# One-core transformer kernel on Trainium2: the first five projection blocks on the unnormed input, scaled in PSUM, and another order of the first transfers

## The reference, cut to what matters

```python
def rms_norm(x, w):
    xf = x.astype(jnp.float32)
    y = xf * lax.rsqrt(jnp.mean(xf * xf, axis=-1, keepdims=True) + EPS)
    return (y * w.astype(jnp.float32)).astype(x.dtype)

def mamba2_mixer(h, norm_w, in_w, conv_w, conv_b, dt_bias, a_log, d_skip, gnorm_w, out_w):
    b, s, _ = h.shape
    u = rms_norm(h, norm_w)
    zxbcdt = u @ in_w
    z, xbc, dt = jnp.split(zxbcdt, [D_INNER, D_INNER + CONV_CH], axis=-1)
    xbc = lax.conv_general_dilated(xbc, conv_w[:, None, :], window_strides=(1,),
    ...
    xbc = jax.nn.silu(xbc)
    ...
    dt = jax.nn.softplus(dt.astype(jnp.float32) + dt_bias.astype(jnp.float32))
    a = -jnp.exp(a_log.astype(jnp.float32))
    y = ssd_chunked(xs, dt, a, bm, cm)
```

## Time and profile before

| | |
|---|---|
| median of three runs | 1540.54 us (1541.24, 1516.41, 1540.54) |
| the profiled execution | 1513.08 us |
| its span | 1511.2 us |
| mean granted TensorE clock | 0.971 |
| PE busy | 1413.0 us |
| DVE, ACT, POOL busy | 817.0, 649.1, 659.5 us |

### The profile page before, as it was taken

How to read it: one execution, slowest core, us unless ns; L and a number is a source line. 1 busy time by engine, 2 the same in 40 slices (tenths; PEclk the granted TensorE clock), 3 DMA queues, 4 the chain that set the end, 5 groups by cost and what they waited for, 6 DMA issues and landing times.

```text
span 1511.2 us, 18102 instructions
## 1 busy us (share of the span) xinstructions
PE 1413.0 (94%) x6802; PEld 1114.1 (74%) x6802; DVE 817.0 (54%) x1358; ACT 649.1 (43%) x1090; POOL 659.5 (44%) x319
## 2 busy tenths in 40 slices
PE   5989999999999999789999999988989999999996
PEld 4877878777678788556887888664558788888775
DVE  4535564757566734664675311356646554455656
ACT  4634524535444534584554311444544332332452
POOL 3443453535334544355544334323244455555441
PEclk9999999999999999999999999988999999999998
DMA  4221222222223233110323343120003233333331
GB/s 160 86 70 56 84 71 77 77 70 69 72 70 97 71 98 92 35 56 29 92 90 114 96 137 128 56 71 1 1 1 98 84 98 98 98 98 98 98 94 60
DMA packets 33366, 118.92 MB, mean 79 GB/s; under 512 B 3964, under 2 KB 4348, under 8 KB 33024
## 3 DMA queue, kind: packets, MB, share of 16 engines
q1 hardware_dynamic: 31680, 113.26, 24.2%
q10 hardware_dynamic: 1600, 4.50, 0.9%
HBM read 115.65 MB, written 2.10 MB: 78 GB/s over the span
## 4 chain that ended last, share of the span: by engine, by line
PE 76%; DVE 10%; ACT 8%; issue 4%; POOL 2%; ACTq 0%; DMA 0%; DVEq 0%
PE bank L1153 73%; DVE arena L1817 2%; PE bank L1535 1%; ACT wsh L786 1%; ACT arena L1087 1%; ACT sq L749 1%; POOL wsl L641 1%; DVE h L1818 1%; ACT arena L917 1%; POOL arena L720 1%; PE bank L1389 1%; DVE arena L1813 1%; DVE arena L1656 1%; DVE arena L1637 1%; DVE arena L2125 0%
## 5 line engine op out<-in xcount | busy, mean ns | idle before, releaser
L641 POOL TENSOR_TENSOR wsl<-ring,wsh 128x1024 fp32r<-128x1024 f32 x199 | 482.8, 2427 | 670.9 <-ACT wsh L786 670.9
L786 ACT ACTIVATE wsh<-ring 128x1024 fp32r<-128x1024 f32 x199 | 210.3, 1057 | 557.7 <-PE bank L1153 513.6
L1153 PE MATMUL bank<-parts0h,wsh 128*128 128x512 f32 x744 | 301.4, 405 | 15.2 <-DVE small L1920 4.4
L1153 PE MATMUL bank<-parts0h,wsl 128*128 128x512 f32 x744 | 292.9, 394 | 0.0
L1153 PE MATMUL bank<-parts0l,wsh 128*128 128x512 f32 x744 | 292.9, 394 | 0.0
L1153 PE MATMUL bank<-parts1h,wsh 128*128 128x512 f32 x688 | 275.0, 400 | 6.7 <-POOL parts1l L641 3.1
L1153 PE MATMUL bank<-parts1l,wsh 128*128 128x512 f32 x688 | 269.5, 392 | 0.0
L1153 PE MATMUL bank<-parts1h,wsl 128*128 128x512 f32 x688 | 269.4, 392 | 0.0
L1153 PE MATMUL bank<-arena 128*64 128x128 f32 (+10 forms) x1008 | 168.2, 398 | 28.8 <-DVE arena L2165 7.9
L1153 PEld LDWEIGHTS bank<-parts0h,wsh 128*128 128x128 f32 x744 | 141.7, 190 | 55.2 <-issue 10.2
L1153 PEld LDWEIGHTS bank<-parts0l,wsh 128*128 128x128 f32 x744 | 141.9, 191 | 31.0 <-issue 2.6
(11 more groups left out here) (279 smaller groups left out, 1870.8 us busy)
## 6 DMA issues: line engine op xcount, KB each, us to landing
ring<-in_wstream SPq DMA_DIRECT2D x210, 512.0 KB, 3.6
arena<-in_alibi ACTq DMA_DIRECT2D x2, 1024.0 KB, 5.1
outT<-arena SPq DMA_DIRECT2D x8, 256.0 KB, 2.1
h<-in_xT SPq DMA_DIRECT2D x2, 512.0 KB, 6.1
h<-in_xT ACTq DMA_DIRECT2D x2, 512.0 KB, 6.3
arena<-in_cmpb ACTq DMA_DIRECT2D x1, 496.0 KB
con<-in_con ACTq DMA_DIRECT2D x1, 390.5 KB
rowb<-in_rowb ACTq DMA_DIRECT2D x1, 184.0 KB
```

Source lines behind the costliest of these rows:

```text
L641: return nc.gpsimd.tensor_tensor(dst, src, hi.bitcast(F32), ALU.subtract)
L786: nc.scalar.activation(wsh[n % NSET][:, :], src, ACT.Copy).then_inc(*done("high", ("high", L)))
L1153: return nc.tensor.matmul(*args, **kw)
```

## The change

Blocks p00, p01, dt, p02 and p03 no longer use the normed input. ACT and DVE split `h * norm weight` straight into pair 1 (step `raw`), PE multiplies these, and the factor is put on the product: DVE multiplies the PSUM bank in place by `rtb0`, a copy of the spread factor in SBUF, before the convolution or the copy to `dtf` reads it. The matmuls of the five blocks stand at new steps `("L", ...)` ahead of the old ones; what ACT and DVE do with the products stays at the old steps. The squares, the column sums and the spread of the factor follow behind or between these blocks, and the normed input is made in two halves (`("hn", "ssm", 0)` and `1`), first used by p04. The first two weight blocks get their low part from DVE, not POOL. The first transfers are reordered: on ACT's queue `vec` goes first, then two quarters of the input; on SP's queue weight block 0, then the other two quarters, then the stream. The copies `identr` and `laterr` move to the step `cum`, behind p03, since they lie in pair 1.

```diff
--- before.py
+++ after.py
@@ -91,6 +91,10 @@
 VERSION_OF = {"ssm": 0, "ple0": 1, "kv": 2, "attn": 2, "ple1": 3, "ln1": 4, "ln2": 5, "ple2": 6, "final": 7}
+RAW = [("proj", 0, 0), ("proj", 0, 1), ("dtl",), ("proj", 0, 2), ("proj", 0, 3)]
+LATER = RAW + [("upg", 0), ("upv", 0)]
 def pipeline(x, units, closing):
...
@@ -116,7 +120,8 @@
 def steps():
-    out = [("load",), ("norm", 0), ("first_weights",), ("nb", 0), ("hn", "ssm")]
+    out = [("first_weights", 0), ("raw",), ("first_weights", 1), ("load",)] + [("L", *x) for x in RAW[:2]]
+    out += [("norm", 0), ("nb", 0), ("hn", "ssm", 0), ("L", *RAW[2]), ("hn", "ssm", 1)] + [("L", *x) for x in RAW[3:]]
     proj = {g: [("proj", g, i) for i in range(10)] for g in range(GROUPS)}
     sout = {g: [("sout", g, m) for m in range(KD)] for g in range(GROUPS)}
     out += proj[0][:2] + [("dtl",), proj[0][2], ("dt",), proj[0][3], proj[0][4], ("cum",)] + proj[0][5:7] + [("angles",)] + proj[0][7:]
...
@@ -392,7 +397,7 @@
 def splits_at(step):
     if step[0] == "first_weights":
-        return [(b, SPLITNO[b]) for b in SPLIT[:NSET]]
+        return [(SPLIT[step[1]], step[1])]
...
@@ -615,12 +624,11 @@
         @block.sync
         def _(sp):
-            for m in range(0, KD, 4):
-                sp.dma_start(h[:, m:m + 2, :], ins["xT"][:, m:m + 2, :])\
-                    .then_inc(*done(f"xin{m}", ("h", 0, m), ("h", 0, m + 1), inc=16))
-            sp.wait_ge(*at("h", 0, 4))
             for L, b in enumerate(BLOCKS):
+                if L == 1:
+                    for m in range(2, KD, 4):
+                        sp.dma_start(h[:, m:m + 2, :], ins["xT"][:, m:m + 2, :])\
+                            .then_inc(*done(f"xin{m}", ("h", 0, m), ("h", 0, m + 1), inc=16))
...
@@ -722,19 +730,21 @@
         @block.scalar
         def _(act):
-            for m in range(2, KD, 4):
+            act.dma_start(vec[:, :], ins["vec"]).then_inc(*done("vec_in", ("vec",), inc=16))
+            for m in range(0, KD, 4):
                 act.dma_start(h[:, m:m + 2, :], ins["xT"][:, m:m + 2, :])\
                     .then_inc(*done(f"xin{m}", ("h", 0, m), ("h", 0, m + 1), inc=16))
-            for i, (dst, name) in enumerate([(con[:, :], "con"), (vec[:, :], "vec"), (rowb[:, :], "rowb"),
-                                             (w2c[:, :, :], "w2c"),
+            for i, (dst, name) in enumerate([(con[:, :], "con"), (rowb[:, :], "rowb"), (w2c[:, :, :], "w2c"),
                                              (peT[:, :, :], "peT"), (mbias[:, :], "mbias"), (pos[:, :], "pos")]):
-                act.dma_start(dst, ins[name]).then_inc(*done("consts", *([("consts",)] if i == 6 else []), inc=16))
+                act.dma_start(dst, ins[name]).then_inc(*done("consts", *([("consts",)] if i == 5 else []), inc=16))
...
-                    nc.scalar.activation(identr, ident, ACT.Copy)
-                    nc.scalar.activation(laterr, later, ACT.Copy).then_inc(*done("mask_parts", ("mask_parts",)))
+                if k == "raw":
+                    for m in range(KD):
+                        act.wait_ge(*at("h", 0, m))
+                        nc.scalar.activation(xgh[:, m, :], h[:, m, :], ACT.Identity,
+                                             scale=vec[:, V_NORM["ssm"] + m:V_NORM["ssm"] + m + 1])\
+                            .then_inc(*done("rawhi", ("rawhi", m)))
...
                     b = ps(step)
-                    act.wait_ge(*at("mm", *step))
+                    act.wait_ge(*at("raw_scaled" if step in RAW else "mm", *step))
...
                 if k == "cum":
+                    act.wait_ge(*at("mm", *RAW[-1]))
+                    nc.scalar.activation(identr, ident, ACT.Copy)
+                    nc.scalar.activation(laterr, later, ACT.Copy).then_inc(*done("mask_parts", ("mask_parts",)))
                     act.wait_ge(*at("mm", "lg"))
...
@@ -1166,13 +1181,17 @@
                               skip_group_check=True)
                 return last
-            def linear(job, name, src, normed=None):
+            def linear(job, name, src, normed=None, middle=None):
                 b = open_bank(job)
                 w = weights(name)
                 for kt in range(KD):
-                    if normed:
+                    if normed == "raw":
+                        pe.wait_ge(*at("raw", kt))
+                    elif normed:
                         pe.wait_ge(*at("hn", normed, kt))
+                    if middle and kt == KD // 2:
+                        middle()
                     last = mm3(b[:, :], [q[:, tok(kt)] for q in w], [q[:, kt, :] for q in src], kt == 0, kt == KD - 1)
...
                     b = open_acc(("ss", a[0]))
...
-                    b = open_acc(("rb", a[0]))
-                    pe.wait_ge(*at("ndiag", a[0]))
-                    mm(b[:, :], ones, rt[:, :], start=True, stop=True).then_inc(*done("mm", ("mm", "rb", a[0])))
-                if k == "proj":
-                    linear(step, blocks_of(step)[0], hn, "ssm" if a == (0, 0) else None)
-                if k == "dtl":
-                    linear(step, ("dt",), hn)
+                def broadcast(ver):
+                    b = open_acc(("rb", ver))
+                    pe.wait_ge(*at("ndiag", ver))
+                    mm(b[:, :], ones, rt[:, :], start=True, stop=True).then_inc(*done("mm", ("mm", "rb", ver)))
+                if k == "nb" and a[0]:
+                    broadcast(a[0])
+                if k == "proj" and step not in RAW:
+                    linear(step, blocks_of(step)[0], hn, "ssm" if a == (0, 4) else None)
...
                         linear(step, blocks_of(step)[0], hn)
-                if k == "L":
+                if k == "L" and a in RAW:
+                    linear(a, blocks_of(step)[0], xg, "raw" if a == RAW[0] else None, (lambda: broadcast(0)) if a == ("dtl",) else None)
+                if k == "L" and a not in RAW:
                     linear(a, blocks_of(step)[0], hn, "ln2" if a == ("upg", 0) else None)
...
                         .then_inc(*done("split_p", ("split", L), ("slot_free", L)))
+                if k == "first_weights":
+                    b, n = splits_at(step)[0]
+                    L = BLKNO[b]
+                    dve.wait_ge(*at("high", L))
+                    low(wsl[n % NSET][:, :], ring[:, L % NSLOT, :], wsh[n % NSET][:, :])\
+                        .then_inc(*done("split_first", ("split", L), ("slot_free", L)))
+                if k == "raw":
+                    dve.wait_ge(*at("vec"))
+                    for m in range(KD):
+                        dve.wait_ge(*at("rawhi", m))
+                        nc.vector.scalar_tensor_tensor(xgl[:, m, :], h[:, m, :], vec[:, V_NORM["ssm"] + m:V_NORM["ssm"] + m + 1],
+                                                       xgh[:, m, :].bitcast(F32), ALU.mult, ALU.subtract)\
+                            .then_inc(*done("raw", ("raw", m)))
+                if step in RAW:
+                    dve.wait_ge(*at("rtb", 0))
+                    dve.wait_ge(*at("mm", *step))
+                    nc.vector.tensor_tensor(ps(step)[:, :], ps(step)[:, :], rtb0, ALU.mult)\
+                        .then_inc(*done("raw_scaled", ("raw_scaled", *step)))
...
                             .then_inc(*done("hn_dve", ("hn", name, q)))
+                if k == "nb" and a[0] == 0:
+                    dve.wait_ge(*at("mm", "rb", 0))
+                    nc.vector.tensor_copy(rtb0, acc(("rb", 0))[:, :]).then_inc(*done("rtb", ("rtb", 0)))
...
```

More of the change, by code:

```diff
@@ L253, in jobs_of @@
         return [a]
-    if step in (("upg", 0), ("upv", 0)):
+    if step in LATER:
         return []
@@ L328, in blocks_of @@
     if k == "L":
-        return [(*a, 0)]
-    if step in (("upg", 0), ("upv", 0)):
+        k, a = a[0], a[1:]
+    elif step in LATER:
         return []
@@ L533, in build @@
         rtb = ar(38, SEQ)
+        rtb0 = ar(25, SEQ)
         rtb1 = ar(35, SEQ)
@@ L538, in build, with tiles_of @@
         hf3 = [ar(30 + b, SEQ) for b in range(4)]
+        def tiles_of(a):
+            return list(range(KD)) if len(a) == 1 else list(range(4 * a[1], 4 * a[1] + 4))
         def normed_tiles(name):
@@ L648, in _ @@
                     src = ring[:, L % NSLOT, :]
-                    if n is not None:
+                    if n is not None and k != "first_weights":
                         pool.wait_ge(*at("high", L))
@@ L653, in _ @@
                 if k == "hn" and a[0] != "final":
-                    for name in a:
+                    for name in a[:1]:
                         hi, lo = (xgh, xgl) if name == "kv" else (hnh, hnl)
                         buf = normed_tiles(name)
-                        for m in range(1, KD, 2):
+                        for m in tiles_of(a)[1::2]:
                             pool.wait_ge(*at("hnhi", name, m))
@@ L737, in link @@
                 act.wait_ge(*at("act_step", chain[0]))
+            act.wait_ge(*at("vec"))
             def square(ver, m):
@@ L804, in _ @@
                 if k == "hn" and a[0] != "final":
```

(19 more changed lines are left out.)

## The result

| | before | changed |
|---|---|---|
| first comparison, median of 4 runs each | 1528.47 us (1512.5 to 1541.24) | 1539.24 us (1537.29 to 1541.11) |
| second comparison (with r1 to e3 below) | 1517.15 us (35 runs) | 1531.39 us (12 runs) |
| fourth comparison (with r2, e8, e9) | 1523.61 us (29 runs) | 1541.33 us (12 runs) |

What follows compares the result with a forecast made beforehand. PE bounds the kernel (busy 1413.0 of 1511.2 us); an 11.0 us lead, less 9.2 us idle at the transposes and 1.8 us half pace, sums to +0.4 us: 1541 us in the upper place, range 1508 to 1546.

Steps and rivals of the forecast that it cites:

- the sum: Opening stage to p04's end: 59.4 us against 59.0 before, so +0.4 us, put on the upper place's 1540.5 us.
- the two places of the runs: Whole kernel: runs at 1516.41 or 1540.54 to 1541.24 us, by something not the change's; median forecast in the upper.
- The head: Start through p03: p00 starts at 9.9 us instead of 23.12, p03 ends at 42.6 instead of 53.6, lead 11.0 us.
- The transfers: First loads of input and weights: their new order costs nothing, since the bytes are the same.
- The transposes: After p03: PE idle for 9.2 us while ACT and DVE work one after the other towards `dtf`, leaving 1.8 us lead.
- The product in place in PSUM: DVE's products on the path to `dtf`: 0.69 us each, bounds 0.43 us and twice 0.69.
- The half pace: p04 behind the idle gap: nine matmuls at 0.43 instead of 0.227 us, 1.8 us lost, p04 ends at 59.4 us.
- the other half of the working: Behind p04: if PE kept its pace, `cum` would wait for `da` until 58.8 us, so half pace costs only 0.6 us.
- Rival A: Transposes: ACT and DVE reach `dtf` without PE's gap, the lead stays, 11 us shorter, 1529.5 us; it or half, chance 0.10.
- Rival B: Normed tiles: DVE and POOL in each other's way, POOL's block up to 3.70 us, p03 late, +2.5 us, 1543 us; chance 0.09.

Runs made afterwards that it cites:

- r1: The changed kernel rerun unaltered; 6 of 12 runs at 1540.41 to 1543.24 us, the others 1514.86 to 1522.38 us.
- e3: Changed kernel with dt's product and copy and p00's product and first tap ahead of p03; 7 of 12 runs over 1530 us, lower five median 1511.75 us.
- r2: The changed kernel rerun unaltered a third time; 8 of 12 runs over 1530 us, the four lower runs with median 1520.3 us.
- e8: Changed kernel without 24 of the 40 one-column sums of the mLSTM, denominators incomplete; median 1511.33 us, 12 runs from 1504.39 to 1512.74.
- e9: Kernel before with seven extra ACT activations ahead of the squares; 6 of 12 runs over 1530 us, the six lower with median 1520.6 us.
- e1: Changed kernel with 16 extra unread 128x512 matmuls at the start of the mLSTM product stage; median 1518.45 us, none of 12 runs over 1530.
- e2: Kernel before with 16 extra unread 128x512 matmuls at the start of the mLSTM product stage; median 1517.0 us, none of 12 runs over 1530.
- e5: Kernel before with three extra ACT activations ahead of the squares; 8 of 12 runs over 1530 us, the four lower with median 1518.6 us.
- e6: Kernel before with only the new order of the first transfers; p00 starts at 25.94 us, 2.8 later; 4 of 12 runs over 1530 us.
- e4: Changed kernel with 16 filler matmuls in the mLSTM stage and 36 more ahead of PE's wait for the transposes; median 1517.56 us, 0 of 12 over 1530.
- e7: e3's step order with 8 filler matmuls in the mLSTM stage; median 1510.93 us, ratio to the lower runs of before 0.9966.

## Why the prediction was wrong

**The step that failed** is one sentence of the sum: that the two places of the runs come "by something that the rows don't show and that isn't the change's". From it the forecast took one fixed place for both kernels, and so +0.4 us between them; the spell had no term. That it isn't the change's stands as far as the runs show; that it could be held fixed, the same on both sides, is what failed. What the runs showed in its place: the places are a spell at half pace in the mLSTM stage, 64.9 us or 3.4 us long, that each kernel falls into in some of its executions and not in others. The change's four runs all fell in the upper place, two of before's four did, and so the first comparison has the change 1.5% slower than the low runs of before, while without the spell (e1, e2) it is +1.45 us. That 1539.24 us lies only 1.8 us from the forecast is luck: four draws of four in the place that I had named.

Could the rows have shown it? In part. Before the forecast I had windows of 30 us over the whole span of before, and they read a granted clock of 0.94, 0.78, 0.78 and 0.86 between 960 and 1080 us. I used the windows of the first 100 us only, for what they meant for the change. But 90 to 120 us reads 0.89 as well, part of the low clock behind 1010 us lies beside an idle PE, and there was no trace of an upper run, so the rows gave a stage to suspect and not the cause. The two places in three runs were reason enough for a term of up to 25 us either way, with a chance.

Whether the change also makes the spell likelier is open. Over all comparisons 18 of 28 runs of the changed kernel were upper and 36 of 103 of before. Taken as independent runs that would be chance in about 1 of 100 cases; but within a comparison they share a chip, and the first four alone were what raised the question (without them 14 of 24 against 34 of 99, 1 in 27). Delays at the start (e5, e9) gave 14 of 24, the reorder e3 7 of 12, e6 with a delay of 2.8 us 4 of 12. There is no rule of the delay in these. What isn't open is that the spell needs no change to appear.

**The head** was right: 9.9 us forecast, 10.18 measured; the end of p01 23.0 (22.8), the column sums 1.7 us (1.9), p03 late by 0.5 us (0.34 us of it idle by PE's record) and its end 42.9 (42.6). In r1, r2, e1 and e8 PE stays longer at half pace at its start, and p03 ends at 43.2 to 44.4. The transfers cost nothing, as reasoned, in this kernel; e6 shows that they cost 2.8 us where the constants are wanted early.

**The transposes** were right: forecast 9.2 us of idle PE, measured 9.22. The product in place in PSUM takes 0.69 us, the row with one PSUM operand, not twice that. The same wait is 9.21 or 9.22 us in all five traces of this order. e3 shows that the queue order is the cause.

**The half pace** was mis-sized in the trace above, and the sum with it. I took nine matmuls from the start's 4.0 us. There it lasted until 58.4, thirteen matmuls at 0.43 us (not fifteen, as e4's expectation has it), and p04 took 8.3 us instead of 5.45: 2.9 us lost instead of 1.8. In r1, r2, e1 and e8 p04 took 7.0, 7.3, 8.4 and 7.1 us, so 1.8 lies inside a scatter of 1.5 to 3.0. But where this stretch is short the one at the start is long, and p04 ends at 60.4 to 61.5 in all five, against 59.4 forecast: +1.3 to +2.4 us for the stage, not +0.4. The size of one stretch can't be read from another; this term needed a range, and the one at the start too. e4 confirms the other half of the working: with PE kept at its pace `cum` waits for `da` until 58.9 (58.8 forecast).

**Rival A** (the lead stays) is out: it took another order of the steps to get 5.0 of the 11 us. **Rival B** did not come by its own path: POOL's block took 2.39 us, not 3.70, and p03 was late by 0.5 us. But DVE was stretched more than its row. The timeline, DVE and POOL:

```profile
34.85 2.77 DVE L1614 TENSOR_TENSOR parts0l<-arena,parts0h 128x512 fp32r<-128x512 f32 x1
```
```profile
34.68 2.39 POOL L649 TENSOR_TENSOR wsl<-ring,wsh 128x1024 fp32r<-128x1024 f32 x1
```

The low part of tile 4 began 0.17 us behind POOL's block and took 2.77 us, where the earlier trace rows had let me expect 1.68 and the other low parts here took 0.69: it ended 0.55 us behind the end of POOL's (37.07). The Trainium skill, "SBUF — State Buffer", section "Who interferes with whom", states that a DVE instruction with two SBUF inputs contends with a GpSimd instruction that reads SBUF, and that the shared ports are held exclusively. The measured number agrees. It cost nothing, since DVE was done at 40.3 us and ACT could not use it before 43.9.

## What to carry to other kernels

A head start on one engine is worth only what the engines behind it can follow: list what is queued in front of the first step that PE waits for, and move that step's inputs, here the copy of one block, ahead of the blocks that don't need it. Where the runs of a kernel lie in two places, find the stage before costing a change: compare granted clock and matmul count, not busy time, of a high and a low run in windows. And compare two such kernels either over many runs or with the spell taken out of both; cheap matmuls in the wait ahead of the stage did that here, eight in e7 and sixteen in e1, e2 and e4.

## What the runs showed of the hardware that I had not expected

A stage in which PE is busy without a gap can stay at the 1.2 GHz level: granted clock 0.50 from 963.0 to 1027.9 us in the first trace of the change, while PE was busy for all of 970 to 1030. Three traces have this spell, of 64.9 us each. The work there is fp32 products with one-column sums between them, and then the first 5 us of a projection block. With 24 of the 40 sums left out (e8) none of 12 runs was in the upper place, and with 8 or 16 dense 128x512 matmuls in the wait ahead (e1, e2, e4, e7) none of 48. The clock can also fall without a wait: in e1 at 977.3 us, for 3.4 us, while PE was busy. The same program, unaltered, does or doesn't have the long spell on different runs, at a price of 25 us in 1515.

How long PE stays at half pace, at its start and behind a gap of 9.2 us, differs between executions of one and the same code: behind the gap seven to fourteen matmuls in five traces.
